# Attention outputs kept by features and divided through rows in memory; order of work shifted in attention and at the start

## The reference, cut to what matters

```
h = rms_norm(x, mix_norm_g); proj = h @ w_in
aq, ak, av, hq, hf, hi, hg = split(proj)
attn = softmax(rms_norm(aq) rms_norm(ak)^T * 64**-0.5 + bias, over 9 chunks of 64 keys) @ av
x = x + concat(attn, hgrn_out) @ w_out
x = x + 0.5 * swiglu_ffn(rms_norm(x, ffn2_norm_g))
```

## Time and profile before

| | |
|---|---|
| three timed runs | 1884.92, 1885.41 (median), 1886.67 us |
| the profiled execution | 1885.16 us, of which the span is 1883.6 us |
| granted TensorE clock | 1.00 of full speed over the span |
| PE busy | 1869.4 us (99%) |
| DVE, ACT, POOL busy | 1125.0, 675.3, 406.7 us |
| attention | from about 1030 to 1144 us of the span |
| output projection | from 1145.06 us |

### The profile page before, as it was taken

One profiled execution on the slowest core, in us unless ns is written; L12 is line 12 of the kernel. 1 busy time (PEld: TensorE's weight loads), 2 busy tenths in 40 slices (PEclk: granted clock), 3 DMA queues, 4 the chain that ended last, 5 costly groups with the idle time before them and its releaser, 6 DMA issues. The chain is left out here.

```text
span 1883.6 us, 24459 instructions
## 1 busy us (share of the span) xinstructions
PE 1869.4 (99%) x9171; PEld 1546.3 (82%) x9171; DVE 1125.0 (60%) x1591; ACT 675.3 (36%) x1029; POOL 406.7 (22%) x319
## 2 busy tenths in 40 slices
PE   9999999999999999999999999999999999999999
PEld 8888888888888888888888678888888888888887
DVE  6966665665546641156667874477666656655464
ACT  7422323333333533211223663353223233333332
POOL 2043422241103110002222310000434222411030
PEclk9999999999999999999999999999999999999999
DMA  5355444436866433434433510133554444368653
GB/s 182 112 196 190 146 162 168 153 138 244 318 195 197 131 122 124 138 101 140 134 132 106 162 60 1 68 112 112 196 190 146 163 167 153 138 244 306 219 192 140
DMA packets 221341, 296.52 MB, mean 157 GB/s; under 512 B 15377, under 2 KB 117913, under 8 KB 221234
## 3 DMA queue, kind: packets, MB, share of 16 engines
q1 hardware_dynamic: 206752, 262.19, 41.0%
q0 software_dynamic: 6272, 18.14, 3.0%
q10 hardware_dynamic: 8210, 14.75, 2.0%
HBM read 206.13 MB, written 92.56 MB: 159 GB/s over the span
## 5 line engine op out<-in xcount | busy, mean ns | idle before, releaser
L710 PE MATMUL ps<-hThi,whi 128*128 128x512 f32 x888 | 346.6, 390 | 0.2 <-DVE hid L1751 0.2
L712 PE MATMUL ps<-hThi,wlo 128*128 128x512 f32 x888 | 345.5, 389 | 0.0
L711 PE MATMUL ps<-hTlo,whi 128*128 128x512 f32 x888 | 345.5, 389 | 0.0
L710 PE MATMUL ps<-whi 128*128 128x512 f32 x616 | 240.0, 390 | 0.0
L712 PE MATMUL ps<-whi,wlo 128*128 128x512 f32 x616 | 239.7, 389 | 0.0
L711 PE MATMUL ps<-wlo,whi 128*128 128x512 f32 x616 | 239.6, 389 | 0.0
L710 PEld LDWEIGHTS ps<-hThi,whi 128*128 128x128 f32 x888 | 166.7, 188 | 34.9 <-issue 0.9
L712 PEld LDWEIGHTS ps<-hThi,wlo 128*128 128x128 f32 x888 | 166.7, 188 | 34.7
L711 PEld LDWEIGHTS ps<-hTlo,whi 128*128 128x128 f32 x888 | 166.7, 188 | 34.3
L710 PE MATMUL ps<-hXhi,whi 128*128 128x512 f32 x480 | 186.9, 389 | 0.8 <-issue 0.8
L712 PE MATMUL ps<-hXhi,wlo 128*128 128x512 f32 x480 | 186.8, 389 | 0.0
(11 more groups left out here) (220 smaller groups left out, 2828.7 us busy)
## 6 DMA issues: line engine op xcount, KB each, us to landing
hid_scratch<-hid SPq DMA_DIRECT2D x132, 256.0 KB, 3.3
raw<-ffn_w_gate SPq DMA_DIRECT2D x44, 512.0 KB, 3.8
raw<-ffn_w_up SPq DMA_DIRECT2D x44, 512.0 KB, 4.9
wdb<-ffn_w_down SPq DMA_DIRECT2D x44, 512.0 KB, 4.1
wd_scratch<-wdb SPq DMA_DIRECT2D x88, 256.0 KB, 4.3
raw<-hid_scratch SPq DMA_DIRECT2D x80, 256.0 KB, 2.8
rawx<-hid_scratch SPq DMA_DIRECT2D x74, 256.0 KB, 2.8
raw<-w_in SPq DMA_DIRECT2D x28, 512.0 KB, 5.4
```

The source lines that it names most:

```text
L710: pe.matmul(dst, ahi, bhi, start=first, stop=False, skip_group_check=onto)
L711: pe.matmul(dst, ahi, blo, start=False, stop=False, skip_group_check=onto)
L712: return pe.matmul(dst, alo, bhi, start=False, stop=last, skip_group_check=onto)
```

## The change

Attention's outputs stay with features on the partitions. `keep_out` writes them to catT, and they are neither turned back nor turned again: `turn_out` and `head_output` go. Since the division is by a number per token, which now runs along the row, the inverse sums have to lie along rows, the same in 64 partitions. `invert_sums` inverts the sums of a pair (of half a pair in the last), `store_rcp` writes them to rcp_d in memory, word by word, `load_rcp` reads them back as rows spread over 64 partitions for each head into rowr, and `norm_out` multiplies catT by rowr in place, for pairs 0 to 2 at units 9 and 11 of the pair after. The recurrent outputs have a tile of their own, cath, and only they are turned for the output projection: four blocks per tile (`turn_cat`), four tiles ahead, in PSUM banks 0 to 3. `cat_hi` and `cat_lo` take the place of `hT_hi` and `hT_lo` there, with two instructions each, one from PSUM (cath) and one from catT.

Shifts of order: squares and sums of q and k at units (1, 3) and (2, 4) of a pair in place of (1, 4) and (3, 5); `take_half` of halves 0 and 3 ahead of the exponential of its unit; at the beginning four idle products in place of six ahead of the first product, and `weight_lo(0, 0)` before `early_lo_part(2, 0)`. Three semaphores of one small chain (`lb_diff`, `lb_sig`, `lb_ready`) become one. The rest of the diff is declarations.

```diff
@@ -163,7 +163,8 @@
...
 NV = NU * PAIRS
-SQUARE_AT, SUM_AT, NORM_AT = (1, 4), (3, 5), (6, 8)
+SQUARE_AT, SUM_AT, NORM_AT = (1, 3), (2, 4), (6, 8)
@@ -302,8 +302,8 @@
...
     psumr = keep("psumr", [P, 2, 2, TT], where=c)
-    rcp = keep("rcp", [P, 2, 2, TT], where=c)
-    outT = keep("outT", [P, 2, T], where=c)
+    rcp = keep("rcp", [P, 2, TT, 2], where=c)
+    rowr = keep("rowr", [P, 2, T], where=c)
 with ExitStack() as c:
@@ -320,7 +320,9 @@
...
 with ExitStack() as c:
-    cat = keep("cat", [P, TT, D], where=c, side="right")
+    catT = keep("catT", [P, PAIRS, T], where=c, side="right")
+    cath = keep("cath", [P, TT, HALF], where=c, side="right")
 qin = y[:, 1, :].rearrange("p (t c) -> p t c", t=TT)
@@ -666,6 +667,26 @@
...
                      .rearrange("(t p) c -> p t c", p=P)).then_inc(av_loaded[p % 2], 16)
+    def store_rcp(p, g=None):
+        tiles = slice(0, TT) if g is None else slice(4 * (1 - g), 4 * (1 - g) + 4)
+        sp.wait_ge(rcp_ready, p + 1 + (g or 0))
+        sp.dma_start(rcp_d[p, tiles].rearrange("t h p -> p (t h)"),
+                     rcp[:, p % 2, tiles, :].rearrange("p t h -> p (t h)"),
+                     allow_slow_non_contiguous=True).then_inc(rcp_stored, 16)
+    def load_rcp(p, g=None):
+        tiles = slice(0, TT) if g is None else slice(4 * (1 - g), 4 * (1 - g) + 4)
+        sp.wait_ge(rcp_stored, 16 * (p + 1 + (g or 0)))
+        if p >= 2:
+            sp.wait_ge(out_normed, 2 * (p - 2) + 2)
+        for hd in range(2):
+            row = rcp_d[p, tiles, hd:hd + 1, :].rearrange("t h p -> h t p")
+            sp.dma_start(rowr[hd * DH:(hd + 1) * DH, p % 2, tiles.start * P:tiles.stop * P]
+                         .rearrange("r (t p) -> r t p", p=P),
+                         row.to_broadcast([DH, tiles.stop - tiles.start, P])).then_inc(row_loaded, 16)
     out_pieces(0)
@@ -684,9 +705,16 @@
...
         load_qk(p)
+        store_rcp(p - 2)
         sp.wait_ge(unit_out, NU * (p - 1))
...
         load_v(p)
+        load_rcp(p - 2)
+    store_rcp(PAIRS - 2)
+    load_rcp(PAIRS - 2)
+    for g in range(2):
+        store_rcp(PAIRS - 1, g)
+        load_rcp(PAIRS - 1, g)
     for t in range(TT):
@@ -752,20 +776,17 @@
...
         mm.then_inc(turned, 1)
-    def turn_cat(t, h):
-        if h and t == 0:
+    def turn_cat(t):
+        if t == 0:
             pe.wait_ge(cat_loaded, 16)
             pe.wait_ge(unit_max, NV)
-        elif h == 0 and t == 0:
-            pe.wait_ge(head_out, 2 * PAIRS - 1)
-        c0 = turn_bank(R_CAT, t) * HALF + h * HALF
+        elif t >= 4:
+            pe.wait_ge(hT_ready, TT * R_CAT + t - 3)
         for k in range(4):
-            at = h * HALF + k * P
-            mm = pe.transpose(ps[:, c0 + k * P:c0 + (k + 1) * P], cat[:, CAT_ORDER[t], at:at + P], ident[:, :])
-        if h == 0:
-            mm.then_inc(turned, 1)
+            mm = pe.transpose(ps[:, cat_bank(t) * HALF + k * P:cat_bank(t) * HALF + (k + 1) * P],
+                              cath[:, CAT_ORDER[t], k * P:(k + 1) * P], ident[:, :])
+        mm.then_inc(turned, 1)
     def early_turn(t, h):
@@ -878,7 +899,7 @@
...
             idle_products(2)
-    idle_products(6)
+    idle_products(4)
     products(0, 0, 1)
@@ -1066,47 +1087,17 @@
...
         mm.then_inc(unit_out, 2)
-    def wait_half_bank(what, p, n):
-        if what == "qk":
-            if n:
-                pe.wait_ge(qkT_ready, 4 * p + n)
-            elif p > 1:
-                pe.wait_ge(head_out, 2 * (p - 2) + 2)
-        elif n == 0:
-            if p < PAIRS - 1:
-                pe.wait_ge(qkT_ready, 4 * p + 8)
-            else:
-                pe.wait_ge(head_out, 2 * (p - 1) + 2)
-        else:
-            pe.wait_ge(head_out, 2 * p + 1)
     def turn_half(p, n):
         pe.wait_ge(qk_normed, 2 * p + n // 2 + 1)
-        wait_half_bank("qk", p, n)
+        pe.wait_ge(qkT_ready, 4 * p + n)
         for t in range(4):
...
         mm.then_inc(qk_turned, 1)
-    def turn_out(p, g):
-        pe.wait_ge(outT_ready, NU * p + (NU - 4 if g == 0 else NU))
-        wait_half_bank("out", p, g)
-        for t in range(4):
-            c0 = (4 * (1 - g) + t) * P
-            b = 7 * HALF
-            mm = pe.transpose(ps[:, b + t * P:b + (t + 1) * P],
-                              outT[:, p % 2, c0:c0 + P], ident[:, :])
-        mm.then_inc(out_turned, 1)
     def halves(w, place):
-        p, step = w // OUT_STEPS, w % OUT_STEPS
-        if place == 0:
-            for g in range(2):
-                for q in range(PAIRS - 1 if g else PAIRS):
-                    if out_step(q, g) == w:
-                        turn_out(q, g)
+        p, step = w // (NU // 2), w % (NU // 2)
         if p + 1 < PAIRS:
@@ -1125,19 +1116,19 @@
...
         if w == STEPS:
-            turn_cat(0, 1)
-            turn_cat(1, 1)
+            turn_cat(0)
+            turn_cat(1)
         if 1 <= w <= STEPS:
...
         if w == STEPS + 1:
-            turn_cat(0, 0)
+            turn_cat(2)
         if w >= 2:
...
         halves(w, 1)
-    turn_cat(1, 0)
+    turn_cat(3)
     for h in range(2):
@@ -1146,7 +1137,7 @@
...
             if h == 0 and t == 2:
-                pe.wait_ge(head_out, 2 * PAIRS)
+                pe.wait_ge(outT_ready, NV)
             if 8 * h + t >= 4:
@@ -1168,10 +1159,8 @@
...
             mm.then_inc(row_done, 1)
-            if d == 0:
-                turn_out(PAIRS - 1, 1)
-            if h == 0 and t + 2 < TT:
-                turn_tile(R_CAT, t + 2)
+            if h == 0 and t + 4 < TT:
+                turn_cat(t + 4)
             if h == 1 and t >= 1:
@@ -1212,14 +1201,20 @@
...
         c0 = turn_bank(R, t) * HALF
-        if R == R_CAT:
-            if t == 0:
-                act.wait_ge(unit_out, NV)
-            t = CAT_ORDER[t]
-        elif R == R_MIX:
+        if R == R_MIX:
             t = MIX_ORDER[t]
...
         act.activation(hThi[:, :, t * P:(t + 1) * P], src, ACT.Copy).then_inc(hT_hi_ready, 1)
+    def cat_hi(t):
+        act.wait_ge(turned, TT * R_CAT + t + 1)
+        if t == 0:
+            act.wait_ge(unit_out, NV)
+        at = slice(CAT_ORDER[t] * P, (CAT_ORDER[t] + 1) * P)
+        act.activation(hThi[:, 4:KT, at], bank(cat_bank(t)).rearrange("p (k c) -> p k c", k=4), ACT.Copy)
+        act.wait_ge(out_normed, 2 * PAIRS - (1 if t < 4 else 0))
+        act.activation(hThi[:, 0:4, at], catT[:, :, at], ACT.Copy).then_inc(hT_hi_ready, 1)
     def early_hi_part(t, h):
@@ -1517,11 +1512,9 @@
...
         act.wait_ge(unit_out, 2 * w + 2)
-        if p >= 2 and 2 * w % NU == 0:
-            act.wait_ge(out_turned, 2 * (p - 2) + 2)
         for q, (t, n, c0) in enumerate(parts):
             b = 6 * HALF + q * P
-            last = act.activation(outT[:, p % 2, t * P:(t + 1) * P], ps[:, b:b + P], ACT.Copy)
+            last = act.activation(catT[:, p, t * P:(t + 1) * P], ps[:, b:b + P], ACT.Copy)
         last.then_inc(outT_ready, 2)
@@ -1536,33 +1529,35 @@
...
             take_turned(v - 2)
-        if v < NV - NU and v % NU == TURN_QK_AT[3][2]:
-            take_half(v // NU + 1, 3)
+        if v < NV - NU:
+            for n in (0, 3):
+                if TURN_QK_AT[n][2] == v % NU:
+                    take_half(v // NU + 1, n)
         if v < NV:
...
             if p >= 2 and v % NU == 0:
-                act.wait_ge(rcp_ready, 2 * (p - 2) + 2)
+                act.wait_ge(rcp_ready, p - 1)
             for t, n, c0 in parts:
...
         if v < NV - NU:
-            for n in range(3):
+            for n in (1, 2):
                 if TURN_QK_AT[n][2] == v % NU:
...
         if v == NV + 2:
-            hT_hi(R_CAT, 0)
+            cat_hi(0)
         if v >= 4 and v % 2 == 0:
...
     for t in range(1, TT):
-        hT_hi(R_CAT, t)
+        cat_hi(t)
     for q in range(4):
@@ -1644,15 +1639,21 @@
...
         c0 = turn_bank(R, t) * HALF
-        if R == R_CAT:
-            t = CAT_ORDER[t]
-        elif R == R_MIX:
+        if R == R_MIX:
             t = MIX_ORDER[t]
...
                           hThi[:, k0:KT, t * P:(t + 1) * P].bitcast(F32), ALU.subtract)\
+           .then_inc(hT_ready, 1)
+    def cat_lo(t):
+        dve.wait_ge(hT_hi_ready, TT * R_CAT + t + 1)
+        at = slice(CAT_ORDER[t] * P, (CAT_ORDER[t] + 1) * P)
+        dve.tensor_tensor(hTlo[:, 4:KT, at], bank(cat_bank(t)).rearrange("p (k c) -> p k c", k=4),
+                          hThi[:, 4:KT, at].bitcast(F32), ALU.subtract)
+        dve.tensor_tensor(hTlo[:, 0:4, at], catT[:, :, at], hThi[:, 0:4, at].bitcast(F32), ALU.subtract)\
            .then_inc(hT_ready, 1)
@@ -1881,8 +1882,8 @@
...
     early_lo_part(1, 0)
+    weight_lo(0, 0)
     early_lo_part(2, 0)
-    weight_lo(0, 0)
     early_lo_part(3, 0)
@@ -2098,17 +2099,22 @@
                   lambda: norm_qk(0, 1)])
-    def head_output(p, g):
-        tiles = slice(4 * (1 - g), 4 * (1 - g) + 4)
-        dve.wait_ge(unit_exp, NU * p + (NU if g else NU - 4))
-        dve.reciprocal(rcp[:, p % 2, :, tiles], psumr[:, p % 2, :, tiles]).then_inc(rcp_ready, 1)
```

(72 more changed lines are left out.)

14 lines of the change are left out of this document (3 added, 11 removed).

## The result

The changed kernel takes 1896.85 us (median of 5 runs, 1895.01 to 1901.77) against 1885.03 (5 runs, 1884.92 to 1886.67) of the kernel before: a ratio of 1.0062 [1.0051, 1.0073]. Forecast were 1880.2 and a range up to 1883.8. The profiled execution took 1895.33 us.

What follows compares the result with a forecast made beforehand. PE, busy 1869.4 of 1883.6 us, was taken to bound the kernel, with VectorE's maxima close beside it. Terms summed to a 5.2 us gain: 1885.16 - 5.2 = 1880.0, plus 0.25 gives 1880.2; range 1876.2 to 1883.8.

Steps and rivals of the forecast that it cites:

- step 6: Handover: store and loads through memory take 8.2 us against 8.7 at hand, just in time; gain 0.4 us.
- step 5: norm_out at units 9 and 11: VectorE idles there and rows have long landed; nothing, at most 0.1 us per pair.
- Rival C: Handover: single-word store lands as late as the 15.2 us row, PE stalls 9.9 us, kernel slower at 1890; chance 0.06.
- Step 1: After the handover: transposes that vanish from PE, less the four turn_cat that come in; net gain 3.8 us.
- Step 2: Attention: vanished transposes cut first steps of pairs 1 to 3 from 4.58 to 3.91, gain 2.0; last pair gains 0.45.
- Step 3: Attention: sums moved between the maxima make second steps about 1.1 us longer, third steps 4.14 us; net loss 2.8 us.
- Rival A: Attention: the moved sums are hidden, giving 3.8 us more gain, 1876.4 us; chance 0.15.
- Step 4: Attention: take_half(0) before the exponential removes PE's 0.40 us wait for qT, three times; gain 1.2 us.
- Step 7: Beginning: two idle products fewer and weight_lo(0, 0) moved up start the first product sooner; gain 0.15 us, between 0 and 0.3.

Runs made afterwards that it cites:

- eleventh kernel: Changed kernel with single words stored at pitches of 16, 32 and 8 B (pairs 0 to 2), 4 and 16 B (last pair's halves); 1891.92 us.
- the first experiment: Changed kernel with each partition's inverse sums stored as one run of 64 B (32 B for a half) instead of single words; 1881.73 us.
- the third experiment: Kernel before with only squares and sums moved to units (1, 3) and (2, 4); 1889.96 us against 1885.37, ratio 1.0027.
- the sixth: Changed kernel with inverse sums turned on PE and stored as rows, squares and sums back at (1, 4) and (3, 5); 1877.42 us.
- 9: Kernel before with only four idle products instead of six, weight_lo(0, 0) earlier, and take_half of halves 0 and 3 before the exponential; 1885.07 us, ratio 0.9996.
- the seventh kernel: Changed kernel with pair 2's two norm_out moved from units 9 and 11 of the last pair to behind the loop; 1899.13 us.
- the eighth: Changed kernel with the last pair's two word stores issued from ScalarE's queue, the first 6.6 us behind pair 2's loads; 1901.16 us.
- the fourth: Changed kernel with words at pitches of 64, 512 and 4 B (pairs 0 to 2), 32 and 128 B (last halves), rows 64 KB apart; 1895.44 us.
- 2: Changed kernel with squares and sums put back at units (1, 4) and (3, 5); 1892.26 us, ratio 1.0033 to the kernel before.
- 10: Changed kernel with the last pair's word stores from ScalarE's queue, the first before its unit's exponential, 3.8 us behind pair 2's loads; 1903.51 us.
- the fifth: Changed kernel with inverse sums transposed on PE, copied by ScalarE and stored as rows of 512 B; 1881.82 us, ratio 0.9981 to the kernel before.

## Why the prediction was wrong, step by step

Two steps failed: step 6, which mis-sized the store, and step 5, which put the wait for the rows at nothing.

**Step 6, the failed one.** The store of 1024 single words was sized at 4.8 us, from a *load* of 1024 single words. It takes 10.7 to 11.1. The row was of the right count and the right size of access, in the wrong direction; the trace of before had no store of single words at all. The rule of the Trainium skill (DMA: Bandwidth & Descriptors, "Rules for kernel authors") that I quoted, one descriptor per element, named the danger without a price. The estimated 2.0 us of the fit in the Trainium skill (the same page, "Anatomy of one DMA"), which is given there for DMAs that GpSimd issues and not SyncE, missed by 9 us: the measurement decides. By the prediction's own sum a store of 11.0 makes 14.4 us of the 8.2, which against the 8.7 at hand is a stall of 5.7. The eleventh kernel shows this error by itself: pair 2's rows come in time there, the last pair's words are at 4 B (11.0 us), PE waits 7.43 us before the projection, and the handover takes 17.85 us for 11.10, 6.75 more.

Rival C had the right suspicion, that such a store lands as late as a slow rearrangement, and I gave it 0.06, with "nothing but the kind of access" for it. That was the only argument that counted, and it was one about something no row showed. That its 9.9 us of stall are near the 9.04 measured is luck: it took 15.2 us for the store and put the stall in front of the first row, while the 9.04 stand before the turns of `cath` and come from pair 2's rows, the subject of step 5.

**Step 5, "its rows have long landed".** The wait came first here, not at the handover. I gave pairs 0 and 1 some 14 us from the store's issue; they used 19.1 (1065.55 to 1084.68) and 18.9, and pair 2 used 23.1. I had counted one transfer of the usual size where there are a store and then loads, and the loads are late as well: 6.7 to 7.2 us for pairs 0 and 1, where bias and v_in, themselves held up by the word store, still land at 1080.1 and 1082.2 (pair 0), and 11.1 for pair 2's second load, with a word store behind it; I had 3.2, for a half. A whole pair's loads with nothing beside them take 3.7 and 4.3 us in the first experiment. Pair 2, whose rows made the longest wait, I had not looked at. The prediction did write down the consequence ("all maxima behind it would wait") and priced it at nothing. It made 2.67 + 2.11 + 9.51 us of waits of VectorE. In the attention row they are most of the 3.1 us between +2.63 and the -0.49 of the first experiment: the sixth step of pair 1 takes 5.73 and of pair 2 5.04, for 4.36 before (together 2.05), and the fifth steps take 5.36 and 5.84 for the 5.03 of pair 0 (1.14), ScalarE's late start (last section) among their causes.

**The handover's sum.** 11.10 us, as it is when the store is fast, + 9.04 of PE idle + 1.9 at the lower clock = 22.0; measured 22.16.

**Step 1 held:** -3.75 for -3.8. Where the earlier trace rows had eight transposes at 0.87 between rows of products, the chain of the changed kernel has four at 0.44.

**Step 2 held:** the first steps of pairs 1 to 3 take 3.91, 3.92 and 3.92 us for a forecast 3.91, and the last pair is dense.

**Step 3 held in mechanism and size.** The second step of a pair takes 4.87 in pair 0 and 4.98 in pairs 1 and 2 (forecast 3.76 + 1.1 and 3.91 + 1.08), the third 4.14 in all (forecast 4.14). The order of time of the changed kernel beside the earlier trace rows:

```profile
1090.99 1.35 PE L1052 MATMUL ps<-kT,qT 64*128 64x512 f32 x8
1092.37 0.82 DVE L2129 CUSTOM_DVE_ANT_0 S<-ps,bias 128x640 f32<-128x640 f32 x1 [1.61 <-PE ps L1052]
1093.86 1.21 DVE L2088 TENSOR_REDUCE ssq<-junk 128x16 f32<-128x1024 f32 x1
1094.98 0.24 DVE L2108 RECIPROCAL rcp<-psumr 128x16 f32<-128x16 f32 x1
1095.14 0.76 DVE L2129 CUSTOM_DVE_ANT_0 S<-ps,bias 128x640 f32<-128x640 f32 x1
1095.97 1.35 PE L1052 MATMUL ps<-kT,qT 64*128 64x512 f32 x8 [0.99 <-DVE nmax L2129]
```

1095.97 - 1090.99 = 4.98, and PE waits 0.99 for the maximum behind the sum and the inverse. Rival A is refuted by this, by the third experiment (+4.3 in attention in the kernel before) and by the sixth (some 3.8 for putting it back).

**Step 4 held in the place, not quite in size:** 0.33 to 0.34 us a pair in the fifth steps that rows do not spoil, for 0.4, and the sixth steps take 4.40 for 4.36.

**Step 7 can't be told from nothing.** The first product comes at 14.77 instead of 15.12, 0.35 us sooner for a forecast 0.15; ahead of it PE waits 1.2 us in two stops for VectorE's xs, where it waited 0.25 before. At the first scores -0.09 is left, and in the kernels of experiments 1 and 9 they come 0.39 and 0.55 later than before. But they come 0.46 later in the third too, whose edit lies behind them, so a few tenths at this place say nothing of the edit. What makes that spread between programs ahead of attention is left open.

**In sum.** Without the store's landing the forecast of -5.2 would have been -4.2 in the span of the first experiment, which took 3.6 us less than the kernel before by the medians. Of the miss of 16.7 us, 15.1 are the landing, with the loads it held up and 1.9 us of clock (1896.85 to 1881.73). By the two traces it is 13.7: 11.1 at the handover and 3.1 in attention, less 0.5 ahead of it. The other 1.5 are 1.0 of terms mis-sized (0.5 ahead of attention, 0.4 in it, 0.05 each at the handover and behind it) and 0.5 by which the gain over the kernel before is smaller in the medians than in the spans.

## What to carry to other kernels

A transfer that no row shows is sized by the nearest row of its own direction; where there is none, its worst end belongs into the likeliest case if a chain of waits ends on it. Behind a store that a load must follow, count store, load and the place in the queue, and look at what stands behind the waiting instruction on its engine. To bring a few hundred numbers from partitions into rows, turn them on PE and store runs: here one transpose and one copy of a thin tile cost 0.1 us of the step they stand in, and single words at a 4 B pitch cost some 10 us of landing each time.

## What the runs showed of the hardware

Single words of 4 B, 16 to a 64 B stretch, complete 9 us after the last of their packets in the trace (1125.8 to 1134.95; the same for 1024 words, 1154.8 to 1163.89). The Trainium skill (DMA: Bandwidth & Descriptors, "Specifications") says that below 512 B a DMA engine does a read-modify-write; runs of 64 B are below that too and landed in 1.4 us, so the size alone isn't the price. Other transfers in flight can suffer: bias and v_in issued right behind a word store landed in 14.1 and 15.3 us, before in 4.1 and 5.1, and behind the runs of the first experiment in 4.3 and 5.4.

ScalarE started `take_half` 1.06 us late in pair 2 of the changed kernel (the wait is put down to neither engine nor data: "remote"), after an idle stretch of 2.00 us in the seventh kernel, of 2.40 in the eighth and of 2.75 in the fourth. Such waits stand in attention in all six kernels that store whole pairs' words at a 4 B pitch in it (the changed one, 2, 4, 7, 8 and 10), each begins while such a store is still to land, and in none of the other seven. What the engine waits for then is not settled here.

The granted clock fell to 0.50 not only after idle stretches: in the fifth and the seventh kernel it was 0.50 for some 3 us in pair 0 (around 1041 and 1040), where PE had been at work but for a wait of 1.04 us.
